# The last pair of experts taken out of the loop, its token sum accumulated in PSUM onto the residual

## The reference, cut to what matters

```python
x = layernorm(ALPHA * x + mixer(x), ln1_g, ln1_b)
logits = x @ router_w + router_b                  # (264, 32); top 4, softmax over them
for e in range(32):                               # rows that chose expert e, at most 64 a pass here
    hgu = x_rows @ w_gu[e] + b_gu[e]              # 1024 -> 2048
    gate, up = min(hgu[:, :1024], 7), clip(hgu[:, 1024:], -7, 7)
    act = (up + 1) * gate * sigmoid(1.702 * gate)
    y[rows] += weight * (act @ w_down[e] + b_down[e])
out = layernorm(ALPHA * x + y, ln2_g, ln2_b)
```

## Time and profile before

| | |
|---|---|
| median of 3 runs | 1373.86 us |
| the three runs | 1371.49, 1373.86, 1374.36 us |
| span of the profiled execution | 1371.4 us (its other time is not given apart; the lowest run is 1371.49 us) |
| PE busy | 1193.2 us (87%) |
| DVE busy | 393.0 us (29%) |
| ACT busy | 280.8 us (20%) |
| HBM traffic, mean | 333 GB/s; 416 to 419 GB/s in the slices of the expert loop |
| granted TensorE clock, mean | 0.969 |

### The profile page before, as it was taken

How to read it: one execution, slowest core, us unless ns; L and a number is a source line. 1 busy time by engine, 2 the same in 40 slices (tenths; PEclk the granted TensorE clock), 3 DMA queues, 4 the chain that set the end, 5 groups by cost and what they waited for, 6 DMA issues and landing times.

```text
span 1371.4 us, 18353 instructions
## 1 busy us (share of the span) xinstructions
PE 1193.2 (87%) x7063; PEld 632.8 (46%) x7063; DVE 393.0 (29%) x645; ACT 280.8 (20%) x424; POOL 212.1 (15%) x120
## 2 busy tenths in 40 slices
PE   5986799988769999998989889898988989898895
PEld 5885667788634443343333334333333433333342
DVE  4948414483552202122020212202020220202026
ACT  3574334333240110111101010111101011110101
POOL 4674444466520000000000000000000000000000
PEclk9998899999879999999999999999999999999998
DMA  9543234554569999999999999999999999999991
GB/s 304 163 126 111 71 93 142 176 194 155 206 274 407 418 418 416 417 417 419 418 418 418 417 417 417 419 418 419 418 418 417 417 419 418 417 419 418 416 416 69
DMA packets 118385, 457.69 MB, mean 334 GB/s; under 512 B 10376, under 2 KB 49304, under 8 KB 85232
## 3 DMA queue, kind: packets, MB, share of 16 engines
q1 hardware_dynamic: 115200, 445.93, 81.8%
q0 software_dynamic: 3152, 11.31, 2.6%
HBM read 451.25 MB, written 5.95 MB: 333 GB/s over the span
## 4 chain that ended last, share of the span: by engine, by line
DMA 45%; PE 33%; SPq 9%; DVE 7%; issue 3%; ACT 2%; POOL 0%; DVEq 0%; ACTq 0%; POOLq 0%
DMA gu_w<-in_moe_w_gu 44%; PE pool L539 12%; PE pool L736 9%; SPq L399 8%; PE pool L764 3%; PE ub L705 1%; PE ub L637 1%; PE ob L643 1%; DMA dn_w<-in_w_in 1%; PE pool L548 1%; DVE arena L1081 1%; DVE xl_most L1017 1%; PE ob L610 1%; DVE arena L1196 1%; PE ub L618 1%
## 5 line engine op out<-in xcount | busy, mean ns | idle before, releaser
L736 PE MATMUL pool<-gu_w,arena 128*64 128x512 f32 x2048 | 467.2, 597 | 45.8 <-DMA gu_w<-in_moe_w_gu 45.3
L736 PEld LDWEIGHTS pool<-gu_w,arena 128*64 128x64 f32 x2048 | 138.9, 136 | 355.9 <-issue 205.5
L764 PE MATMUL pool<-dn_w,arena 128*64 128x512 f32 x1024 | 226.8, 595 | 21.6 <-ACT arena L990 21.6
L1361 DVE TENSOR_SCALAR arena<-pool 128x512 f32<-128x512 f32 x32 | 22.1, 691 | 767.0 <-PE pool L736 767.0
L539 PE MATMUL pool<-xh,wh 128*128 128x264 f32 x576 | 172.9, 300 | 51.8 <-DVE wl L1023 11.3
L450 POOL TENSOR_TENSOR wl<-dn_w,wh 128x1024 fp32r<-128x1024 f32 x70 | 175.6, 2508 | 159.4 <-ACT wh L801 157.2
L539 PE MATMUL pool<-xh,wl 128*128 128x264 f32 x576 | 168.6, 293 | 0.0
L539 PE MATMUL pool<-xl_most,wh 128*128 128x264 f32 x504 | 148.6, 295 | 0.0
L764 PEld LDWEIGHTS pool<-dn_w,arena 128*64 128x64 f32 x1024 | 70.7, 137 | 157.1 <-issue 127.9
L539 PEld LDWEIGHTS pool<-xh,wh 128*128 128x128 f32 x576 | 114.9, 199 | 58.8 <-issue 44.9
L988 ACT ACTIVATE arena<-arena 128x512 f32<-128x512 f32 x32 | 20.2, 630 | 486.8 <-DVE arena L1361 486.8
(11 more groups left out here) (259 smaller groups left out, 846.9 us busy)
## 6 DMA issues: line engine op xcount, KB each, us to landing
gu_w<-in_moe_w_gu SPq DMA_DIRECT2D x256, 1024.0 KB, 20.5
dn_w<-in_moe_w_down SPq DMA_DIRECT2D x256, 512.0 KB, 21.1
dn_w<-in_w_in SPq DMA_DIRECT2D x24, 1024.0 KB, 5.5
dn_w<-in_w_branch SPq DMA_DIRECT2D x8, 1024.0 KB, 5.2
gu_w<-in_state_gla POOLq DMA_DIRECT2D x8, 512.0 KB, 6.2
out_gla_sample<-gu_w POOLq DMA_DIRECT2D x8, 512.0 KB, 5.2
dn_w<-in_w_o SPq DMA_DIRECT2D x4, 1024.0 KB, 5.1
arena<-in_xT SPq DMA_DIRECT2D x2, 1056.0 KB, 6.1
```

The source lines that it names most:

```text
L736: last = mm(out, xg[:, k, j * CAP:(j + 1) * CAP], gu_w[:, k, cols], start=False, stop=(k == NB - 1))
L764: last = mm(DOWN[s * CAP:(s + 1) * CAP, :], act_t[:, k % 4, k // 4 * CAP:(k // 4 + 1) * CAP], dn_w[:, k, s * HF:(s + 1) * HF], start=(k == ...
L1361: ts(gbuf, GATE, LIMIT, None, ALU.min).then_inc(gclip, 1)
```

## The change

Pair 15 leaves the loop. The loop now runs 15 pairs, and the same `body` is called once more behind it with `final=True` and with a register as the turn number (14 + 1, or later when the further passes have run). In this last body:

- no row is gathered for a following pair (72 products of L705 on PE, the copy L993 on ACT, the choice on DVE), and expert 31 prepares no further one-hot;
- after expert 30's down projection, PE turns the weights of pair 15 and then fills four PSUM banks, those of tiles 0 and 1, by `final_rows`: four products of 128 columns of `yacc` against the identity, and one product of the identity with `x1`, 512 columns wide, both left open to accumulate;
- after expert 31's gate and up have been read, PE does the same for the two halves of tile 2 in the banks `GATE` and `UP`;
- DVE has scaled `x1` by ALPHA before this body (three instructions, `between`), and copies `swT` within it.

Behind it, ACT copies one half of `DOWN` into `eo` and DVE the other; PE's six products add onto the open banks; DVE takes the statistics and the first step of the normalisation directly from PSUM, in the order of tiles 2, 0, 1. The transpositions L778, the sums L1409 and the additions L1427 are gone, and the semaphore `moe_done` with them.

```diff
         def moe_loops(eng, body):
-            with eng.Fori(0, PAIRS) as pair:
+            with eng.Fori(0, PAIRS - 1) as pair:
                 body(pair, pair)
             eng.wait_ge(flag_done, 1)
             over = eng.value_load(flag[0:1, 0:1], min_val=0, max_val=1)
             with eng.If(over == 1):
-                with eng.Fori(1, PASSES) as turn:
-                    with eng.Fori(0, PAIRS) as pair:
-                        body(turn * PAIRS + pair, pair)
+                with eng.Fori(0, PASSES - 1) as turn:
+                    body(turn * PAIRS + (PAIRS - 1), PAIRS - 1)
+                    with eng.Fori(0, PAIRS - 1) as pair:
+                        body(turn * PAIRS + PAIRS + pair, pair)
+            return over * ((PASSES - 1) * PAIRS) + (PAIRS - 1)
...
+FIN = [[ub[:, 0, :], ub[:, 1, :]], [ob[:, 0, :], ob[:, 1, :]], [GATE[0:DEC, :], UP[0:DEC, :]]]
...  PE
+            def final_rows(out, t, s, first, rows):
+                for c in range(4):
+                    mm(out[:, c * P:(c + 1) * P], yacc[:, 4 * s + c, first:first + rows], ident[:, :],
+                       start=(c == 0), stop=False)
+                mm(out, ident[0:rows, 0:rows], x1[0:rows, t, s * HF:(s + 1) * HF], start=False, stop=False)
...
+                    elif final:
+                        pe.wait_ge(gclip, n + 1)
+                        pe.wait_ge(gu_read, n + 2)
+                        for s in range(2):
+                            final_rows(FIN[2][s], 2, s, SEQ, DEC)
                     else:
                         pe.wait_ge(picked, it + 2)
                         pe.wait_ge(scat_read, it * 5 + 6)
                         gather()
...
+                    if final and j == 0:
+                        pe.wait_ge(wpicked, it + 2)
+                        pe.wait_ge(scat_read, it * 5 + 6)
+                        turn_weights(scat_last)
+                        pe.wait_ge(x1_scaled, 3)
+                        for t, s in ((0, 0), (0, 1), (1, 1), (1, 0)):
+                            if (t, s) == (1, 0):
+                                pe.wait_ge(swt_last, 1)
+                            final_rows(FIN[t][s], t, s, t * P, P)
+            body(moe_loops(pe, body), PAIRS - 1, final=True)
-            (the turn of wpick, six units of transpositions L778, six products L786)
+            pe.wait_ge(eo_last, 2)
+            for t in (2, 0, 1):
+                first, rows = TILES[t]
                 for s in range(2):
+                    mm(FIN[t][s], swT[:, first:first + rows], eo[:, s * HF:(s + 1) * HF],
+                       start=False, stop=True).then_inc(last_full, 1)
...  ACT
+                    if final and j == 1:
+                        nc.scalar.copy(eo[CAP:2 * CAP, 0:HF], DOWN[0:CAP, :]).then_inc(eo_last, 1)
+                        return
...  DVE
+            def between():
+                for t, (first, rows) in enumerate(TILES):
+                    ts(x1[0:rows, t, :], x1[0:rows, t, :], ALPHA, None, ALU.mult).then_inc(x1_scaled, 1)
+            at = moe_loops(v, body)
+            between()
+            body(at, PAIRS - 1, final=True)
+            n = at * 2 + 1
+            v.wait_ge(dn_used, n * NB + 2 * NB)
+            V.tensor_copy(eo[CAP:2 * CAP, HF:2 * HF], DOWN[CAP:2 * CAP, :]).then_inc(eo_last, 1)
...
+            def stats(i):
+                t = order[i]                      # order = (2, 0, 1)
+                for s in range(2):
+                    v.wait_ge(last_full, 2 * i + s + 1)
+                    me.done(V.bn_stats(st1[0:rows, t, s, :], FIN[t][s]))
+                (bn_aggr, + EPS as before)
+                for s in range(2):
+                    me.done(stt(y2[0:rows, t, cols], FIN[t][s], mv1[0:rows, t, 0:1], ln2[0:rows, 0, cols],
+                                ALU.subtract, ALU.mult))
+            (finish(i): reciprocal of the root, then one scalar_tensor_tensor over 1024 columns)
+            for i in range(NT):
+                stats(i)
+                finish(i)
...  SP
+            for i, t in enumerate((2, 0, 1)):     # stores in this order
```

More of the change, by code:

```diff
@@ L766, in body @@
                         last.then_inc(dn_used, 1)
[L768 to L773, removed]
-                for s in range(2):
[L775 to L787, removed]
+                    if final and j == 0:
[10 more added lines that the diff above has]
+            for t in (2, 0, 1):
+                first, rows = TILES[t]
+                for s in range(2):
+                    mm(FIN[t][s], swT[:, first:first + rows], eo[:, s * HF:(s + 1) * HF],
+                       start=False, stop=True).then_inc(last_full, 1)
         @block.scalar
@@ L982, in _, with body @@
             nc.scalar.copy(rs[0:1, 0, 0:1], ident[0:1, 0:1]).then_inc(eo_ready, 1)
-            def body(it, pair):
+            def body(it, pair, final=False):
                 for j in range(2):
@@ L990, in body @@
                     nc.scalar.copy(act_t, ACTT.rearrange("p (c s) -> p c s", c=4)).then_inc(actt_ready, 1)
-                    if j == 1:
+                    if j == 1 and not final:
                         sc.wait_ge(gath_done, it + 2)
@@ L1000, in body @@
                     last.then_inc(eo_ready, 1)
[L1002 to L1005, removed]
+            body(moe_loops(sc, body), PAIRS - 1, final=True)
+            for i, t in enumerate((2, 0, 1)):
+                rows = TILES[t][1]
+                sc.wait_ge(y2_var, i + 1)
                 a(rs1[0:rows, 0, t:t + 1], rs1[0:rows, 0, t:t + 1], ACT.Sqrt).then_inc(y2_std, 1)
@@ L1362, in body @@
                     ts(ubuf, UP, LIMIT, -LIMIT, ALU.min, ALU.max).then_inc(gu_read, 1)
-                    one_hot(bass.ds(e + 1, 1))
+                    if not (final and j == 1):
+                        one_hot(slice(e + 1, e + 2) if final else bass.ds(e + 1, 1))
                     if j == 0:
@@ L1406, in _ @@
[L1406 to L1412, removed]
-                rows = TILES[t][1]
-                y = y2[0:rows, t, :]
-                me.done(stt(y, y, mv1[0:rows, t, 0:1], ln2[0:rows, 0, :], ALU.subtract, ALU.mult))
-                v.wait_ge(y2_std, t + 1)
-                me.done(V.reciprocal(rs1[0:rows, 1, t:t + 1], rs1[0:rows, 0, t:t + 1]))
-                me.settle()
-                stt(y, y, rs1[0:rows, 1, t:t + 1], ln2[0:rows, 1, :], ALU.mult, ALU.add).then_inc(y2_done, 1)
```

57 lines of the change are left out of this document (24 added, 33 removed).

## The result

The changed kernel takes 1380.89 us (median of 9 runs, 1374.26 to 1381.92), the kernel before 1373.53 us (9 runs). The ratio is 1.0039, 95% interval 1.0023 to 1.0054: slower, and outside the forecast range of 1370.4 to 1376.8 us. The nine times fall into two groups: six from 1379.8 to 1381.9 us, three from 1374.3 to 1376.0 us. The medians are 7.4 us apart (1.0054); the ratio is that of the means, 5.4 us apart, in which the three low times count. The profiled execution (1381.92 us, span 1380.2 us) is of the upper group. An execution's time lies some 1.7 us above its span in both kernels, so of the 2.5 us by which I carried the sum to the median some 0.8 us (an estimate) are how far the profiled execution of before lay under its median; the forecast difference of -0.8 us is not touched by it.

A forecast was written before the change was run, and what follows sets the result against it. The expert loop was taken as bound by the weights from HBM. Terms +5.7 + 0.95 - 7.45 = -0.8 us took the profiled 1371.4 to 1370.6 us, as a median 1373.1 us; range 1370.4 to 1376.8 us.

The forecast's parts named there:

- the exit of the loop: Moved to before expert 30: TensorE's 0.64 us loss there was to fall into 3.63 us of room, costing nothing.
- the 8.47 us to the down projection's end: From L757 to the end of expert 31's down projection: 8.47 us, taken from the trace before.
- the sum of -0.8 us: Whole kernel: +5.7 + 0.95 - 7.45 = -0.8 us against the profiled execution, 1371.4 to 1370.6 us.
- the room of TensorE: TensorE's slack against the weights' arrival: 3.63 us in expert 30, only 1.79 us in expert 31.
- Ahead of expert 31, +5.7 us: Turning the weights and filling four banks takes TensorE 7.48 us, of which 1.79 us are covered by waiting for weights.
- The Trainium skill's ratio: Load and 128-column product streams: about 81 ns each against 56 alone; the 48 added short passes would cost 2.4 us more.
- That rival: Short passes bound by their weight loads, 189 ns against products of 110: 2.6 up to 6.1 us more; chance 0.13.
- After gate and up, +0.95 us: Behind expert 31's clips, waiting and filling tile 2's two banks takes 4.83 us before L757 instead of 3.86.
- the rival with 0.10: Loop exit under full transfer load stops TensorE beyond expert 30's 3.63 us; each further us lengthens the kernel; chance 0.10.
- point of decision (7.2 us of stop): Exposed stop at the loop exit from which that rival decides: 3.63 + 0.8 + 2.75 = 7.2 us.
- The end, -7.45 us: From the down projection's end to the span's end: 17.9 us instead of 25.35, VectorE being the bound.
- New work that hides, 0.10: Rival: TensorE's new work ahead of expert 31 hides, the 5.7 us fall away, 1367.4 us; chance 0.10.

The follow-up runs named there:

- counted version: Changed kernel, all passes kept, but TensorE reads the flag before its loop and counts its turns instead of jumping over a block: 1375.04 us, 1.0010.
- spread version: Changed kernel with one bank of final rows ahead of expert 31, tile 0's two behind its clips, the rest behind the end's first products; jump kept: 1368.68 us, 0.9963.
- one-body version: Changed kernel with one copy of the body in the skipped block of further passes instead of two: 1380.07 us, 1.0033.

## Why the prediction was wrong, step by step

Two steps failed: the exit of the loop, put at nothing, and the 8.47 us to the down projection's end, carried over at full clock. Between the sum of -0.8 us and the trace's +7.53 us lie 8.3 us: 2.8 us are the stop and the fall behind it, 4.6 us the second fall, and 1.0 us terms that were sized a little low.

**What bounds the kernel, and the room of TensorE: right.** Expert 31's gate and up had no wait for weights and took 14.41 us (1329.38 to 1343.79; 14.39 was read off expert 2).

**Ahead of expert 31, +5.7 us: +6.05.** The banks took 1.75 to 1.85 us each (1.74 in the sum), and the stretch from copy to clip grew from 15.89 to 21.94 us. A pass of 128 columns stepped by 0.11 us: the last of 8 in 1.05 us lasts 0.27. The loads did not show. The Trainium skill's ratio for such streams ("TensorE: Matmul & The Clock Gate", section "Back-to-back issue gap") did not hold here either. That rival is out.

**After gate and up, +0.95 us (4.83 less 3.86 is 0.97): +1.32 at full clock** (5.18 us in the counted version; small gaps between the narrow passes of 128 rows and of 8, which the sum had at nothing), +2.77 in the changed kernel, since its second half ran at 1.2 GHz.

**From there to the down projection's end, 8.47 us carried over unchanged: 11.58.** This step failed. I took every duration at the clock of the trace before and never asked what TensorE would be doing just before it. The edit replaced 3.9 us of dense work by 1.4 us of nothing and narrow passes; the down projection behind it paid 2.64 us. With the small tile's second half and the turn, the second fall cost 4.6 us against the counted version: 1.45 us up to the turn and 3.11 us from there.

**The exit of the loop, costed at nothing, the rival with 0.10: it happened in part.** The stop is 3.3 to 4.5 us, by itself about expert 30's room of 3.63 us, so I had its order right and its point of decision (7.2 us of stop) wrong: what decided was not its length, but that TensorE's clock fell behind it (0.50 over the window of 6.60 us above). That made +2.74 us in expert 30. In the spread version's trace the stop is as long (3.42 us) and the clock held behind it; there the stage from the copy of 29 to the clip of 30 took 17.82 us, as before the change. I read the exit's cost off the idle time that it left, 0.64 us, and not off the branch's own record, which has 3.58 us in the same trace. What the queued products cover, some 3 us, is the same at both places; the branch was 2.4 us longer at the new one. The Trainium skill ("Runtime: NRT & Kernel Launch", section "Instruction fetch mechanics") has the taken branch wait for a fetch when its target isn't loaded. The runs agree in this, that only versions in which TensorE has a block to jump over have the stop, and that the time stands in the branch's record (5.95 us); the fetch itself was not tried apart.

**The end, -7.45 us: -7.15.** Right: VectorE's period was 4.33 us where 4.22 was summed (from tile 0's statistics at 1368.38 to tile 1's at 1372.71), and the last store a large one.

**New work that hides, 0.10: out.** It did not hide, as the room said. Where it can hide is behind the clips and behind the first products of the end, as the spread version shows.

At full clock and without the stop the six stages sum to +0.2 us where I had -0.8, and the counted version measured 1.0 us above the kernel before. The sum was sound for an engine whose speed does not depend on what it did before.

## What to carry to other kernels

A sum made of durations from a trace holds only while TensorE stays as busy as it was there: where an edit takes dense work out of a stretch ahead of something long, price the long thing at half clock too, and put other useful wide work in the gap instead of leaving it. The jump over the code of the further passes cost TensorE 3.6 us in a quiet stretch and 5.9 to 6.2 us beside the weight traffic, of which queued products hid some 3 us; read such a price off the branch's record and not off the idle time, put the jump where nothing waits, or make the trip count a register. Before work is moved off the end, ask which engine is idle at the end: here TensorE was, and the place chosen in front of the last expert had 1.8 us of room for 7.5 us of work.

## What the runs showed of the hardware

Peeling one turn off a loop moved a stop of TensorE that had shown as 0.64 us to a place where it showed as 3.3 to 4.5 us, in all nine traces with the jump (from the copy of expert 29's result to expert 30's first product), and in none of the seven without it. The branch itself took 3.58 us in the trace of before and 5.92 to 6.20 us in the nine. Halving the skipped code did not shorten it (5.99 us, a stop of 3.4 us).

The stop was followed by half clock in eight of the nine traces, during part of expert 30's gate and up; in the spread version's trace, after 3.47 us of idle time, the clock held:

```profile
1288.84 0.62 PE L742 MATMUL pool<-arena,oh 96*64 96x512 bf16 x4 [3.47 <-issue]
```

```profile
1288.80:1303.20 14.40, 14.36 (x69) 5.63 (x70) 0.00 (x0) 0.00 (x0) 0.00 (x0) 1.00 1.01 417
```

2.9 us of idle time behind expert 31's gate and up were followed by a fall in both traces that had them, and both had an earlier fall in expert 30. 1.4 us idle followed by passes on 8 columns were followed by one in all four traces of the changed kernel and in that of the one-body version, and in none of the four traces where neither a stop nor a fall had come before; with 128-column passes behind the same 1.4 us, or with the 1.4 us filled, it held (one trace each, both with the earlier stop and fall). A single execution's trace therefore doesn't tell what such an edit costs: the changed kernel's two groups of times lie some 6 us apart.
